# A decoder step on one core: the entry of layer 0 in one block, dilated attention by head pairs

## The chip, the core and the metric

The kernel runs on one core of one Trainium2 chip. The metric is device time in microseconds (us), as a median over runs. The core has a TensorE (PE) for matrix products, VectorE (DVE), ScalarE (ACT), GpSimd (POOL) and SyncE (SP), each with an instruction row of its own that runs in order; 16 DMA engines move data between DRAM and SBUF (128 partitions). TensorE writes its products into PSUM.

## The reference

One inference step of a two-layer decoder, for a prompt of 1024 tokens and a sample group of 8 sequences of 4 tokens, which share all weights (D_MODEL 1024, float32). Every sub-layer has a root-mean-square norm ahead and is added to its input.

```python
h = rmsnorm(x, norm_mix[layer])
# layer 0, ab_mix
a_lin, a_gate, q, k, v = split_cols(h @ w_in, AB_SPLITS)
a_out, conv_st = conv_module(a_lin * jax.nn.sigmoid(a_gate), conv_hist, ...)
q = rmsnorm(q.reshape(shp), qn)
k = rmsnorm(k.reshape(shp), kn)
for g, (window, dil) in enumerate(zip(WINDOWS, DILATIONS)):   # 128, 512, 2048 by 1, 4, 16
    s = jnp.einsum('nrbqhd,nrbkhd->nrbhqk', qb, kb).astype(F32) * HEAD_DIM ** -0.5 + bias
    s = jnp.where(mask[:, None], s, -jnp.inf)
    o = jnp.einsum('nrbhqk,nrbkhd->nrbqhd', jnp.exp(s - lse[..., None]), vb.astype(F32))
merged = jnp.concatenate([a_out, b_out...], axis=-1)   # @ w_out
```

The three groups of dilated attention have 4 heads of 64 each, blocks of 128 queries against their own and the previous block of keys, and are merged by the softmax of their log-sums. Outputs include the new window caches: for each of the 8 sequences and each group, the old cached keys and values shifted by the 4 new ones (up to 2 MB each in the third group). Layer 1 has gated linear attention beside an indexer-sparse attention with 8 heads: scores over all keys, of which the 256 best of an index stay. For the sample its past keys and values come in pages of 128 tokens. Each layer ends in a SwiGLU feed-forward net.

## The kernel before, in words

The residual stream lies transposed in SBUF: `S.xT`, eight channel tiles k of 128 by T = 1056 tokens, in the first eight rows of `home`. Large products run as three passes over high and low parts of both operands (`Parts`, `passes`), in three pieces of 352 columns (`multiply_pairs`, L364); every weight comes as a raw slice of 512 KB, whose high part ScalarE makes (L336) and whose low part VectorE or GpSimd (L340), with two slots j. The semaphore `W.free[j]` says that slot j of PSUM may be written, `W.product[j]` that its product is done. Small products are plain float32, which count as two TensorE instructions each in the trace; a transpose counts as one.

The program is a chain of blocks. In a block each engine has a hand-written program and they meet in semaphores; between blocks there is a barrier. The order of each row is the order of the code, and DMAs are issued in it from SP's or ScalarE's row.

The entry of layer 0 is four blocks. `load_inputs` (L168) loads the input rows (`xrow`, nine tiles) and 15 small gains on SP, turns x by channel tiles once all rows are in (L205), and copies to `xT` (L217). `bias_lines` (L543) forms relative-position bias lines by a product with one-hot rows (L573, L576), keeps them (L583, L585), stores them, and issues their spread to 128 rows each in DRAM, from which Toeplitz tables are read later. `rms_norm` (L235) squares on ScalarE (L262), sums over channels with a matrix of ones (L284), takes logarithm and exponential (L267, L269), multiplies on VectorE (L307), and splits h in high (L272) and low part, the low parts by turns on VectorE (L301) and GpSimd (L294). The ring between them holds two channel tiles. `glu_products` (L599) turns conv taps and history (L623, L628), then runs four pairs of products; ScalarE takes the sigmoid of slot 0 (L637), VectorE multiplies (L651 to L656).

`qkv_products` (L675) makes q and k of 12 head pairs, one per period, copied by ScalarE (L736), with weights loaded on SP (L328) and the convolution on VectorE (L765 to L772); then the values. `dilated_prompt` (L998) goes over 24 blocks (group g, query block b), 13 of which have one key tile and 11 two. Per block TensorE does scores (L1043), transposes of the probabilities (L1056) and value products (L1066), VectorE the bias (L1083), the row maximum (L1088) and the copy out (L1074), ScalarE the exponentials (L1101) and the copy of the turned probabilities (L1120). ScalarE also issues one cache copy per block (L1113), and SP stores each block's partial rows (L1030), of which four lie in a ring. `dsa_sample` (L2634) has two halves of four sequences each: 16 groups of pages are turned and scored (L2770, L2779), and at a half's end come the new keys and the biases:

```python
                if q % N_PAGES == N_PAGES - 1:
                    ...
                    new_keys_and_bias(q // N_PAGES)      # L2786 to L2793
            turn_probs(0)                                # L2799, L2800
            weigh_values(0)                              # L2810, L2814
            turn_probs(1)
            weigh_values(1)
            turn_out(0)                                  # L2819
```

VectorE takes each half's maximum (L2707), copies turned probabilities (L2711) and adds up heads (`own_heads`, L2721). SP loads pages into the slots that the value products have freed (L2475).

## Time and profile before

| | us |
|---|---|
| three runs | 3776.13, 3785.69, 3785.43 (median 3785.43) |
| the profiled execution: its own time, its span | 3779.81, 3778.0 |
| PE busy (share of the span) | 3154.7 (84%) |
| PE weight loads | 2899.2 (77%) |
| DVE | 1734.0 (46%) |
| ACT | 905.8 (24%) |
| POOL | 128.2 (3%) |

The program has 47856 instructions and moves 257.11 MB. A timeline row gives start, duration, engine, line of the kernel, operation, output<-input and count, and in brackets the engine's idle time before it and what ended that. SPq and ACTq rows are DMA issues. A window row gives each engine's busy time in a stretch and the granted clock of TensorE, where 1.00 is 2.4 GHz and 0.50 is 1.2 GHz. A row of waits gives total us, times and the longest.

### The profile page before, as it was taken

To read this page: it belongs to the slowest core of one execution; us is meant where nothing else is said; L and a number is where in the kernel's file an instruction comes from. 1 tells how busy PE (TensorE), PEld (TensorE's weight loads), DVE (VectorE), ACT (ScalarE), POOL (GpSimd) and SP (SyncE) were. 2 spreads that over 40 slices of the span, in tenths; PEclk is the share of its full clock that TensorE was granted. 3 is DMA by queue.
4 is the path that set the end of the run, shared out by engine and by line. 5 is a ranking of instruction groups with operands and counts; after the bars stand their busy time and mean duration, and the time that the engine had idled before them with its cause. 6 is when DMAs were issued, how large, how long until landed. Compare 5 with 4: busy or idle time off the path is not lost. (4 is left out here: it accounts for less than half of the span.)

```text
span 3778.0 us, 47856 instructions
## 1 busy us (share of the span) xinstructions
PE 3154.7 (84%) x19536; PEld 2899.2 (77%) x19552; DVE 1734.0 (46%) x2434; ACT 905.8 (24%) x1380; POOL 128.2 (3%) x53
## 2 busy tenths in 40 slices
PE   4689778325999999999689844569987999999999
PEld 2689756224999999999479834445664999999998
DVE  1269623453433232333499869373323333232333
ACT  1225324201321111113211141234521322111110
POOL 0112100000000000000012100000000000000000
PEclk7899976655999999999799955679987999999999
DMA  5111137373111111112111000114074111111111
GB/s 180 39 39 39 45 106 247 122 205 96 50 45 50 45 44 45 45 42 82 28 47 48 17 7 13 34 39 131 1 215 151 45 45 45 45 44 45 45 44 69
DMA packets 304496, 257.11 MB, mean 68 GB/s; under 512 B 31313, under 2 KB 279218, under 8 KB 303322
## 3 DMA queue, kind: packets, MB, share of 16 engines
q1 hardware_dynamic: 298079, 223.42, 20.0%
q10 hardware_dynamic: 6300, 32.12, 2.6%
q8 instruction: 75, 1.23, 0.1%
q14 instruction: 42, 0.34, 0.0%
HBM read 226.72 MB, written 62.64 MB: 77 GB/s over the span
## 5 line engine op out<-in xcount | busy, mean ns | idle before, releaser
L364 PE MATMUL ps<-h_given,w_parts_given 128*128 128x352 f32 x6048 | 979.8, 323 | 0.0
L364 PEld LDWEIGHTS ps<-h_given,w_parts_given 128*128 128x128 f32 x6048 | 979.0, 188 | 0.0
L364 PE MATMUL ps<-hidden_ffn,w_parts_given 128*128 128x352 f32 x4176 | 684.2, 326 | 21.2 <-DVE w_parts_given L340 21.2
L364 PEld LDWEIGHTS ps<-hidden_ffn,w_parts_given 128*128 128x128 f32 x4176 | 682.3, 190 | 22.1 <-issue 22.1
L340 DVE TENSOR_TENSOR w_parts_given<-w_given,w_parts_given 128x1024 fp32r<-128x1024 f32 (+2 forms) x154 | 181.9, 1181 | 626.2 <-ACT w_parts_given L336 626.2
L336 ACT ACTIVATE w_parts_given<-w_given 128x1024 fp32r<-128x1024 f32 (+2 forms) x154 | 158.0, 1026 | 914.5 <-PE ps L364 870.8
L1543 DVE TENSOR_TENSOR home<-home,ps 128x1056 f32<-128x1056 f32 (+1 forms) x64 | 80.3, 1254 | 430.4 <-PE ps L364 406.9
L364 PE MATMUL ps<-h_given,w_parts_cd 128*128 128x352 f32 x1152 | 188.4, 325 | 9.7 <-POOL w_parts_cd L340 9.7
L364 PEld LDWEIGHTS ps<-h_given,w_parts_cd 128*128 128x128 f32 x1152 | 188.1, 190 | 9.8 <-issue 9.8
L1998 DVE MATCH_REPLACE8 work<-best,work 128x1024 f32<-128x1024 f32 (+2 forms) x192 | 165.4, 864 | 0.0
L1991 DVE MAX8 best<-work 128x8 f32<-128x1024 f32 (+2 forms) x192 | 154.8, 865 | 0.0
L770 DVE SCALAR_TENSOR_TENSOR yT<-uT,taps,yT 128x1024 f32<-128x1024 f32 x120 | 152.9, 1274 | 0.0
L452 PE MATMUL ps<-h,w_parts_qk 128*128 128x352 f32 x720 | 121.8, 329 | 0.0
L452 PEld LDWEIGHTS ps<-h,w_parts_qk 128*128 128x128 f32 x720 | 116.8, 188 | 4.8 <-issue 4.8
L1502 ACT ACTIVATE hidden_ffn<-home 128x1056 f32 (+1 forms) x44 | 47.8, 1087 | 228.2 <-DVE home L1556 228.2
L792 PE MATMUL ps<-w_parts_qk,h 128*128 128x256 f32 (+1 forms) x648 | 84.2, 295 | 19.0 <-issue 13.8
L792 PEld LDWEIGHTS ps<-w_parts_qk,h 128*128 128x128 f32 (+1 forms) x648 | 82.6, 193 | 21.2 <-issue 14.3
L364 PE MATMUL ps<-h,w_parts_glu 128*128 128x352 f32 x576 | 95.3, 328 | 0.0
L364 PEld LDWEIGHTS ps<-h,w_parts_glu 128*128 128x128 f32 x576 | 95.1, 192 | 0.0
L792 PE MATMUL ps<-w_parts_dv,h_given 128*128 128x256 f32 (+1 forms) x432 | 55.0, 292 | 38.7 <-DVE w_parts_dv L340 35.1
L2540 PEld LDWEIGHTS ps<-diag_dsa,sc_dsa 128*128 128x128 f32 x576 | 70.2, 191 | 21.8 <-issue 20.2
L2540 PE MATMUL ps<-diag_dsa,sc_dsa 128*128 128x128 f32 x576 | 85.3, 289 | 0.2 <-DVE diag_dsa L2596 0.2
(413 smaller groups left out, 3574.8 us busy)
## 6 DMA issues: line engine op xcount, KB each, us to landing
kv_early<-in_cache_dsa_kv SPq DMA_DIRECT2D x92, 256.0 KB, 3.1
w_given<-in_w_ffn_gate SPq DMA_DIRECT2D x44, 512.0 KB, 3.8
w_given<-in_w_ffn_up SPq DMA_DIRECT2D x44, 512.0 KB, 3.8
w_given<-in_w_ffn_down SPq DMA_DIRECT2D x32, 448.0 KB, 3.7
w_cd<-in_w_in_cd SPq DMA_DIRECT2D x20, 512.0 KB, 4.0
w_qk<-in_w_in_ab SPq DMA_DIRECT2D x18, 512.0 KB, 3.8
kv_late<-in_cache_dsa_kv SPq DMA_DIRECT2D x36, 256.0 KB, 3.1
x_spill<-home SPq DMA_DIRECT2D x2, 4224.0 KB, 16.4
```

Of the source, the lines that this page charges most:

```text
L336: act.activation(self.parts.hi[:, 0:kt, j, :], self.raw[:, 0:kt, j, :], ACT.Copy).then_inc(self.hi_made[j], 1)
L340: eng.tensor_tensor(self.parts.lo[:, 0:kt, j, :], self.raw[:, 0:kt, j, :], self.parts.hi[:, 0:kt, j, :], ALU.subtract).then_inc(self.lo_ma ...
L364: last = pe.matmul(S.ps[:, j * 1536 + at:j * 1536 + at + size], w[:, k, j, :], x[:, k, t:t + size], start=k == 0 and n == 0, stop=k == kt ...
L452: last = pe.matmul(S.ps[:, j * 1536 + at:j * 1536 + at + size], w[:, k, j, :], x[:, k, t:t + size], start=k == 0 and p == 0, stop=k == KD ...
L770: dve.scalar_tensor_tensor(yT[:, c, 0:SEQ], uT[:, c, t:t + SEQ], taps[:, c, t:t + 1], yT[:, c, 0:SEQ], ALU.mult, ALU.add).then_inc(conv_st ...
L792: last = pe.matmul(vps[0:m, n % 2, 0:GW], tokens(g, b, x[:, k, :]), w[:, k].rearrange("p j c -> p (j c)"), start=k == 0 and i == 0, stop=k ...
L1502: act.activation(hidden.hi[:, bass.ds(i, 1), :].rearrange("p a t -> p (a t)"), whole, ACT.Copy).then_inc(hi_made, 1)
L1543: dve.tensor_tensor(x, x, slot(S, j), ALU.add).then_inc(W.free[j], 1)
L1991: dve.max(self.best[0:self.rows[j], j, :], line).then_inc(step, 1)
L1998: dve.match_replace(line, self.best[0:self.rows[j], j, :], line, TAKEN).then_inc(step, 1)
L2540: last = pe.matmul(t_ps[:, g % 2, i * P:(i + 1) * P], sc[:, u % 3, b, kt * P:(kt + 1) * P], diag[:, u % 2, b, :], start=True, stop=True)
```

## The change

- **Entry.** The four blocks become one, `entry`. Rows of x are turned, copied, squared and summed by token tiles t, each with a semaphore of its own for its load. Bias-line products come next, then the norm, all of it on VectorE, then the gated products; the first pair follows the low parts k by k. Conv history and taps are turned behind each pair. ScalarE issues the loads of the bias table, the gain of this norm, the one-hot lines and the history at its start, and 13 loads of the other gains behind the high parts, ahead of the first `W.free[0]`. The gated products are unrolled loops. SP stores and spreads the lines between weight loads.
- **q/k products.** ScalarE issues two cache copies per head pair (`copy_cache`), and waits for them at the block's end.
- **Dilated attention.** The unit of turning, copying and weighing is half a block (two heads): turning is a product with the identity, the ring of turned probabilities has four halves instead of two wholes, the value products stand one unit behind, and the cache copies are gone.
- **Sample's sparse attention.** The second half's new keys and biases stand behind the first half's value products; its maximum stands behind `own_heads(0)`.

```diff
...
+def entry(nc, S, W, rows, uT, taps, vS, yT):
...
+            sp.dma_start(S.dsa_line, line_d).then_inc(lines_out, 16)
+            load_weight_pairs(sp, W, KD, CC, w_cols(w, CONV_CH), w_cols(w, 0), there=1)
...
+            def transpose(t):
+                n = N[t]
+                pe.wait_ge(x_in[t], 16)
+                if t >= 2:
+                    pe.wait_ge(evacuated, t - 1)
+                for k in range(KD):
+                    last = pe.transpose(x_ps[:, t % 2, k, 0:n], rows[0:n, t, k * P:(k + 1) * P], S.ident[0:n, 0:n])
+                last.then_inc(transposed, 1)
+            def sum_squares(t):
+                n = N[t]
+                pe.wait_ge(squared, t + 1)
+                for k in range(KD):
+                    last = pe.matmul(sum_ps[:, t * P:t * P + n], S.ones[:, :], sq[:, t % 2, k, 0:n], start=k == 0, stop=k == KD - 1)
+                last.then_inc(summed, 1)
+            pe.wait_ge(ident_in, 16)
+            pe.wait_ge(ones_made, 1)
+            for t in range(QT + 1):
+                transpose(t)
+                if t:
+                    sum_squares(t - 1)
+            sum_squares(QT)
...
+            last.then_inc(lines_product, 1)
+            pe.wait_ge(lines_kept, 2)
+            pe.wait_ge(mean_ready, 1)
+            pe.wait_ge(hist_in, 48)
...
+                multiply_pairs(pe, S, W, KD, 1, S.h, c, made=made_in_order(lo_made, 0) if c == 0 else None)
+                if c:
+                    pe.wait_ge(placed, c)
...
+                act.wait_ge(evacuated, t + 1)
+                if t >= 2:
+                    act.wait_ge(summed, t - 1)
+                act.activation(sq[:, t % 2, :, 0:n], S.xT[:, :, t * P:t * P + n], ACT.Square).then_inc(squared, 1)
...
+                act.activation(S.h.hi[:, k, :], normed[:, k % 2, :], ACT.Copy).then_inc(hi_made, 1)
+            act.dma_start(S.head_ones[:, :], S.c["head_ones"]).then_inc(gains_in, 16)
+            act.dma_start(S.g_mix[:, 1, :], S.d["norm_mix"][1].rearrange("(k p) -> p k", p=P)).then_inc(gains_in, 16)
+            for layer in range(2):
+                act.dma_start(S.g_ffn[:, layer, :], S.d["norm_ffn"][layer].rearrange("(k p) -> p k", p=P)).then_inc(gains_in, 16)
+            for i, name in enumerate(("qn_ab", "kn_ab", "qn_cd", "kn_cd")):
+                for half in range(2):
+                    act.dma_start(S.g_qk[half * DH:(half + 1) * DH, i:i + 1], S.d[name].rearrange("a d -> d a")).then_inc(gains_in, 16)
+            act.dma_start(S.g_gla[:, :], S.d["gla_norm"].rearrange("a v -> v a")).then_inc(gains_in, 16)
+            act.sem_inc(W.free[0], 1)
+            for i in range(CC):
+                if i + 1 < CC:
+                    W.high(act, 0, i + 2, KD)
...
+            dve.wait_ge(rstd_ready, 1)
+            for k in range(KD):
+                if k >= 2:
+                    dve.wait_ge(lo_made, k - 1)
+                dve.scalar_tensor_tensor(normed[:, k % 2, :], S.xT[:, k, :], S.g_mix[:, 0, k:k + 1], rstd, ALU.mult, ALU.mult).then_inc(normalised, 1)
+                if k:
+                    low_part(k - 1)
+            low_part(KD - 1)
+            dve.sem_inc(W.free[1], 1)
...
+def copy_cache(act, S, g, n, out):
+    name, cache = ("win128_s", "win512_s", "win2048_s")[g], S.d[("cache_win128", "cache_win512", "cache_win2048")[g]][0]
+    old = cache.shape[1]
+    keep = min(WINDOWS[g], old + L_NEW) - L_NEW
+    act.dma_start(S.o[name][0, n, 0:keep].rearrange("t a h d -> t (a h d)"),
+                  cache[n, old - keep:old].rearrange("t a h d -> t (a h d)")).then_inc(out, 16)
...
+                for g, n in (divmod(2 * u, N_SEQ), divmod(2 * u + 1, N_SEQ)):
+                    copy_cache(act, S, g, n, cache_out)
...
-        pT = sb("pT", [P, 2, HPG, 256])
+        pT = sb("pT", [P, 4, 2, 256])
...
+            def turn_probs(u):
+                i, f = divmod(u, 2)
+                kts = 2 if has_previous(*blocks[i]) else 1
+                pe.wait_ge(exps, u + 1)
+                if u >= 2:
+                    pe.wait_ge(kept, u - 1)
+                for b in range(2):
+                    for kt in range(kts):
+                        last = pe.matmul(t_ps[:, f, b, kt * P:(kt + 1) * P], sc[:, i % 3, place(2 * f + b), kt * P:(kt + 1) * P], S.ident[:, :],
+                                         start=True, stop=True)
+                last.then_inc(turned, 1)
+            def weigh_values(u):
+                i, f = divmod(u, 2)
+                g, b = blocks[i]
+                kts = 2 if has_previous(g, b) else 1
+                pe.wait_ge(kept, u + 1)
+                if i >= 2 and f == 0:
+                    pe.wait_ge(sums_copied, i - 1)
+                for h in (2 * f, 2 * f + 1):
+                    for kt in range(kts):
+                        v = vS[:, g, b - (kts - 1) + kt, h * DH:(h + 1) * DH]
+                        last = pe.matmul(o_ps[:, i % 2, h * DH:(h + 1) * DH], pT[:, u % 4, h % 2, kt * P:(kt + 1) * P], v,
+                                         start=kt == 0, stop=kt == kts - 1)
+                if f:
+                    last.then_inc(summed, 1)
             scores(0)
             scores(1)
-            for i, (g, b) in enumerate(blocks):
-                pe.wait_ge(exps, i + 1)
-                if i:
-                    pe.wait_ge(kept, i)
-                kts = 2 if has_previous(g, b) else 1
-                for h in range(HPG):
-                    for kt in range(kts):
-                        last = pe.transpose(t_ps[:, h, kt * P:(kt + 1) * P], sc[:, i % 3, place(h), kt * P:(kt + 1) * P], S.ident[:, :])
-                last.then_inc(turned, 1)
-                if i + 2 < len(blocks):
-                    scores(i + 2)
-                pe.wait_ge(kept, i + 1)
-                if i >= 2:
-                    pe.wait_ge(sums_copied, i - 1)
-                for h in range(HPG):
-                    for kt in range(kts):
-                        v = vS[:, g, b - (kts - 1) + kt, h * DH:(h + 1) * DH]
-                        last = pe.matmul(o_ps[:, i % 2, h * DH:(h + 1) * DH], pT[:, i % 2, h, kt * P:(kt + 1) * P], v,
-                                         start=kt == 0, stop=kt == kts - 1)
-                last.then_inc(summed, 1)
+            for u in range(2 * len(blocks)):
+                turn_probs(u)
+                if u % 2 and u // 2 + 2 < len(blocks):
+                    scores(u // 2 + 2)
+                if u:
+                    weigh_values(u - 1)
+            weigh_values(2 * len(blocks) - 1)
...
+            def exponentials(u):
+                i, f = divmod(u, 2)
+                kts = 2 if has_previous(*blocks[i]) else 1
+                if f == 0:
+                    act.wait_ge(row_in, i + 1)
+                for h in (2 * f, 2 * f + 1):
                     last = act.activation(sc[:, i % 3, place(h), 0:kts * P], sc[:, i % 3, place(h), 0:kts * P], ACT.Exp,
                                           bias=row[:, i % 4, h, AT_M:AT_M + 1], accum_out=row[:, i % 4, h, AT_L:AT_L + 1])
-                    if h == HPG - 1:
-                        last.then_inc(exps, 1)
+                last.then_inc(exps, 1)
...
+            def keep_probs(u):
+                i, f = divmod(u, 2)
+                kts = 2 if has_previous(*blocks[i]) else 1
+                act.wait_ge(turned, u + 1)
+                if u >= 4:
+                    act.wait_ge(summed, i - 1)
+                act.activation(pT[:, u % 4, :, 0:kts * P], t_ps[:, f, :, 0:kts * P], ACT.Copy).then_inc(kept, 1)
...
-                name, cache = ("win128_s", "win512_s", "win2048_s")[g], S.d[("cache_win128", "cache_win512", "cache_win2048")[g]][0]
-                old = cache.shape[1]
-                keep = min(WINDOWS[g], old + L_NEW) - L_NEW
-                act.dma_start(S.o[name][0, b, 0:keep].rearrange("t a h d -> t (a h d)"),
-                              cache[b, old - keep:old].rearrange("t a h d -> t (a h d)")).then_inc(cache_out, 16)
...
+            exponentials(1)
+            for u in range(2 * len(blocks)):
+                i, f = divmod(u, 2)
+                if u + 2 < 2 * len(blocks):
+                    exponentials(u + 2)
+                keep_probs(u)
...
-            maximum(1)
             dve.wait_ge(consts, 48)
             keep_probs(0)
+            own_heads(0)
+            maximum(1)
...
-                if q % N_PAGES == N_PAGES - 1:
-                    if q < N_PAGES:
-                        pe.wait_ge(tables_made, 1)
-                        pe.wait_ge(consts, 48)
-                        pe.wait_ge(hot_in, 32)
-                    new_keys_and_bias(q // N_PAGES)
+                if q == N_PAGES - 1:
+                    pe.wait_ge(tables_made, 1)
+                    pe.wait_ge(consts, 48)
+                    pe.wait_ge(hot_in, 32)
+                    new_keys_and_bias(0)
             turn_probs(0)
             weigh_values(0)
+            new_keys_and_bias(1)
...
```

TensorE's row at the entry, before (transposes of x, bias lines, sums over squares, history and taps, first gated pair):

```order
L205 MATMUL ps<-ident,xrow 128x128 x8
L205 MATMUL ps<-ident,xrow 128x32
...
L573 MATMUL ps<-hot,tab 4x383 x2
L573 MATMUL ps<-hot,tab 4x255
L576 MATMUL ps<-hot_dsa,tab 8x512 x2
L576 MATMUL ps<-hot_dsa,tab 8x127
...
L284 MATMUL ps<-vS,ones 128x352 x24
...
L623 MATMUL ps<-ident,home 128x31 x4
L628 MATMUL ps<-ident,home 128x120 x8
...
L364 MATMUL ps<-h,w_parts_glu 128x352 x144
```

And now:

```order
L495 MATMUL ps<-ident,x_rows 128x128 x16
L502 MATMUL ps<-vS,ones 128x128 x8
L495 MATMUL ps<-ident,x_rows 128x128 x8
L502 MATMUL ps<-vS,ones 128x128 x8
...
L517 MATMUL ps<-yT,tab 4x383 x2
L517 MATMUL ps<-yT,tab 4x255
L519 MATMUL ps<-yT,tab 8x512 x2
L519 MATMUL ps<-yT,tab 8x127
...
L234 MATMUL ps<-h,w_parts_glu 128x352 x144
...
L529 MATMUL ps<-ident,home 128x120 x2
L530 MATMUL ps<-ident,home 128x31
```

Sums stand between the transposes of x, and the history behind the pair.

ScalarE's row at the entry, before (squares, first weights' high parts, logarithm and exponential, high parts of h):

```order
L262 ACTIVATE vS<-home 128x1056 x8
L336 ACTIVATE w_parts_glu<-w_glu 128x8x128 x2
L267 ACT_TABLE_LOAD
L267 ACTIVATE vS<-ps,eps 128x1056
L269 ACT_TABLE_LOAD
L269 ACTIVATE vS<-vS 128x1056
L272 ACTIVATE h<-vS 128x1056 x8
...
L336 ACTIVATE w_parts_glu<-w_glu 128x8x128
```

And now:

```order
L547 ACTIVATE vS<-home 128x1024 x8
...
L206 ACTIVATE w_parts_glu<-w_glu 128x8x128 x2
...
L552 ACTIVATE vS<-ps,eps 128x1056
...
L554 ACTIVATE vS<-vS 128x1056
L557 ACTIVATE h<-vS 128x1056 x8
L559 DMA head_ones<-const_head_ones 128x128
L560 DMA g_mix<-in_norm_mix 128x8x1
L562 DMA g_ffn<-in_norm_ffn 128x8x1 x2
L565 DMA g_qk<-in_qn_ab 64x1 x2
...
L566 DMA g_gla<-in_gla_norm 128x1
L206 ACTIVATE w_parts_glu<-w_glu 128x8x128
```

The gain loads, on SP's row before, stand between the high parts of h and the next weights.

TensorE at the start of the dilated attention, before (scores, turning, values by block):

```order
L1043 MATMUL ps<-home 128x128 x4
L1043 MATMUL ps<-home 128x256 x4
L1056 MATMUL ps<-ident,sc 128x128 x4
L1043 MATMUL ps<-home 128x256 x4
L1066 MATMUL ps<-vS,pT 128x64 x4
L1056 MATMUL ps<-ident,sc 128x128 x8
```

And now, by pair of heads:

```order
L1010 MATMUL ps<-home 128x128 x4
L1010 MATMUL ps<-home 128x256 x4
L1022 MATMUL ps<-ident,sc 128x128 x4
L1010 MATMUL ps<-home 128x256 x4
L1036 MATMUL ps<-vS,pT 128x64 x2
L1022 MATMUL ps<-ident,sc 128x128 x4
L1036 MATMUL ps<-vS,pT 128x64 x2
L1022 MATMUL ps<-ident,sc 128x128 x4
L1010 MATMUL ps<-home 128x256 x4
L1036 MATMUL ps<-vS,pT 128x64 x4
```

Between a turn and its values there now stands the next turn.

TensorE at the end of the sample's sparse attention, before (last scores, new keys and biases, turning, values):

```order
L2779 MATMUL ps<-kT,qb_dsa 32x128 x32
L2786 MATMUL ps<-home,qb_dsa 32x32 x16
L2788 MATMUL ps<-dsa_other,ident 128x32
L2792 MATMUL ps<-hot_s,tabr_dsa 128x512 x4
L2793 MATMUL ps<-work_s,dsa_rows 128x512
...
L2799 MATMUL ps<-ident,work 128x128 x8
...
L2810 MATMUL ps<-kv_early,pT_s 32x512 x4
L2810 MATMUL ps<-kv_late,pT_s 32x512 x12
L2810 MATMUL ps<-kv_early,pT_s 32x512 x16
L2814 MATMUL ps<-dv_new,pT_s 32x512 x4
L2799 MATMUL ps<-ident,work 128x128 x8
```

And now:

```order
L2759 MATMUL ps<-kT,qb_dsa 32x128 x32
L2779 MATMUL ps<-ident,work 128x128 x8
...
L2790 MATMUL ps<-kv_early,pT_s 32x512 x4
L2790 MATMUL ps<-kv_late,pT_s 32x512 x12
L2790 MATMUL ps<-kv_early,pT_s 32x512 x16
L2794 MATMUL ps<-dv_new,pT_s 32x512 x4
L2766 MATMUL ps<-home,qb_dsa 32x32 x16
L2768 MATMUL ps<-dsa_other,ident 128x32
L2772 MATMUL ps<-hot_s,tabr_dsa 128x512 x4
...
L2773 MATMUL ps<-new_taken,dsa_rows 128x32
L2779 MATMUL ps<-ident,work 128x128 x8
```

The rows of new keys and biases moved from ahead of the first turn to behind the first values.

## Rows read from the trace of the kernel before

**Rows 1.** Timeline of the entry: start us, us, engine, operation, count, idle before.
```profile
47.65 1.34 DVE L583 COPY line<-ps 4x383 f32<-4x383 f32 x3 [11.43 <-PE ps L576]
...
90.89 2.55 DVE L307 SCALAR_TENSOR_TENSOR vS<-home,g_mix,vS 128x1056 f32<-128x1056 f32 x2 [40.64 <-ACT vS L269]
...
127.39 95.32 PE L364 MATMUL ps<-h,w_parts_glu 128*128 128x352 f32 x576
...
141.22 1.28 ACT L336 ACT_TABLE_LOAD   x1 [28.82 <-PE ps L364]
...
222.75 0.19 DVE L651 TENSOR_TENSOR uT<-ps,home 128x32 f32<-128x32 f32 x1 [19.64 <-PE ps L364]
```

**Rows 2.** Dilated attention: timeline; window with clock, DMA share; waits; issues and landing.
```profile
528.34 2.95 SPq L1024 DMA_DIRECT2D toep<-ab_copies  x6
...
567.49 1.14 PE L1043 MATMUL ps<-home 64*128 64x256 f32 x8
...
576.96 1.04 PE L1056 MATMUL ps<-ident,sc 128*128 128x128 f32 x8
...
580.06 2.00 PE L1066 MATMUL ps<-vS,pT 128*128 128x64 f32 x16
...
680.67 0.50 PEld L1350 LDWEIGHTS ps<-yT,ones 128*128 128x128 f32 x2 [7.52 <-issue]
...
610.00:636.00 26.00, 26.00 (x129) 22.27 (x127) 10.09 (x15) 12.41 (x46) 0.00 (x0) 0.50 0.92 309
...
DVE part_row L1088 <- DMA part_rows<-part_row: 18.9, 3, 12.1
...
L1113 ACTq DMA_DIRECT2D out_win_s<-in_cache_win x24: 517/517/641, 536.0 to 665.8; - x24
...
DMA to landing us min/median/max: 2.8/5.6/14.2
...
DMA to landing us min/median/max: 1.5/3.5/18.4
```

**Rows 3.** Timeline, end of the sample's sparse attention, and SyncE's page loads.
```profile
2825.39 0.49 PE L2786 MATMUL ps<-home,qb_dsa 128*32 128x32 f32 x32
...
2841.77 1.97 PE L2799 MATMUL ps<-ident,work 128*128 128x128 f32 x8
...
2845.52 1.94 PE L2810 MATMUL ps<-kv_early,pT_s 128*32 128x512 f32 x8 [1.57 <-DVE pT_s L2712]
...
2879.06 1.93 PE L2814 MATMUL ps<-dv_new,pT_s 32*32 32x512 f32 x8
...
2830.68 2.57 SPq L2475 DMA_DIRECT2D kv_early<-in_cache_dsa_kv  x3
...
2848.24 1.45 SPq L2475 DMA_DIRECT2D kv_early<-in_cache_dsa_kv  x2
```

**Rows 4.** DMA issues (KB each, median us to landing), and timeline of SyncE's queue.
```profile
xrow<-in_x_prompt SPq DMA_DIRECT2D x8, 512.0 KB, 7.3
...
12.49 4.26 SPq L185 DMA_DIRECT2D g_ffn<-in_norm_ffn  x2
...
16.80 1.23 SPq L188 DMA_DIRECT2D g_qk<-in_qn_ab  x2
```

**Rows 5.** Timeline of TensorE in the prompt's sparse attention.
```profile
2564.08 2.05 PE L2540 MATMUL ps<-diag_dsa,sc_dsa 128*128 128x128 f32 x16 [0.18 <-DVE diag_dsa L2596]
```

**Rows 6.** Windows: stretch, busy us PE PEld DVE ACT POOL, clock, DMA, GB/s.
```profile
16.00:36.00 20.00, 13.29 (x72) 10.80 (x72) 9.68 (x9) 0.00 (x0) 0.00 (x0) 1.00 0.08 1
...
40.00:48.00 8.00, 7.40 (x12) 1.40 (x12) 0.35 (x1) 0.00 (x0) 0.00 (x0) 0.50 0.00 0
```

**Rows 7.** Timeline of the q/k products: ScalarE's copies and a weight load.
```profile
272.32 1.05 ACT L736 ACTIVATE home<-ps 128x1056 f32<-128x1056 f32 x1 [5.58 <-PE ps L452]
...
277.90 0.37 SPq L328 DMA_DIRECT2D w_qk<-in_w_in_ab  x1
...
285.66 1.05 ACT L736 ACTIVATE home<-ps 128x1056 f32<-128x1056 f32 x1 [5.58 <-PE ps L452]
```

In the second group the first row on landing is that of the cache copies, the second that of the stores of partial rows.

333 lines of the change are left out of this document (115 added, 218 removed).

## The prediction

> **What bounds the kernel now.** The busy shares in the table above say TensorE, 84% busy, but a share is an average over stages, so I read the places that the diff touches: the timeline of the entry (before 223 us), of the dilated attention and of the end of the sparse attention for the sample, then the DMA issues, windows over the entry, and the q/k products. All times are of the profiled execution, whose own time is 3779.81 over a span of 3778.0; the median of the three runs is 3785.43, 0.15% above it. With their spread (3776 to 3786) that makes about 0.3% the least change that a measurement of this kernel can tell from none.
>
> In the entry TensorE waits for a chain of blocks: the first gated product starts at 127.39 and ends at 141.2, and from there the products run on until 222.75 [rows 1]. What moves their start moves the rest one for one. In the dilated attention TensorE is busy all through 610 to 636 at a granted clock of 0.50, with DMA at 0.92, and VectorE waits 12.1 us once for a store of partial rows [rows 2]. In the sample's sparse attention the last value pages are asked for one by one as slots come free [rows 3].
>
> **Entry.** Four blocks become one, and transposes, squares and sums go by token tiles of 128 instead of by channel tiles. I rebuild the chain. The first row tile is in at about 5: a tile is 512 KB, and eight issued together had a median of 7.3 us to landing [rows 4], the first well under that. Before, TensorE waited for all nine. A tile then costs 8 transposes and 8 float32 sums. Eight transposes took 1.04 [rows 2]; a float32 product counts as two instructions, and 16 of 128 columns took 2.05 in another place [rows 5]. That is 3.1 per tile, 25 for eight, and about 4 for the first tile's copy and square and the short tile, which nothing hides: the sums end at 34. This needs the upper clock level (2.4 GHz). It stood at 1.00 over 16 to 36 with transposes alone [rows 6]; at 0.50 the tiles would cost 6 each, 20 us more in all.
>
> The Trainium skill (TensorE: Matmul & The Clock Gate, Part 4: PE-mode transpose) says the full clock level doesn't engage for transpose mode. By it the sum would be 20 us longer here. The window with transposes alone at 1.00 [rows 6] differs, and the measurement decides.
>
> The bias-line products, 12 instructions, took 7.40 at 0.50 [rows 6], so about 4 at full clock; I take 5, to 39. VectorE copies them, 1.34 for the three narrow ones [rows 1] and as much for the wide one: to 42. The logarithm and the exponential on ScalarE run beside this and end no later. The norm is now on VectorE alone: two multiplies take 2.55 [rows 1], and a subtraction has the same size, so 1.27 each. The eighth multiply is the 14th instruction of its row: 42 + 14 x 1.27 = 60. TensorE could follow the low parts from 44.5 on, were it not for a new gate. ScalarE frees slot 0 only behind the eighth high part, for which it waits until that multiply, and behind the issues of 13 gain loads. Two loads of 1024 single words took 4.26 to issue, two half columns 1.23 [rows 4], so 3 x 2.1 + 8 x 0.62 + 1.0 = 12.3 us, to 72. Nothing hides them: TensorE waits there, with VectorE done at 62.
>
> The first product then takes 13.8 as before, since TensorE comes to it from rest in both kernels: to 86, where it was 141.2, so 55 earlier. The history transposes, formerly ahead of the products, stand behind each pair, 4 x 0.9 of the gain back. Net **-52**. Bounds: -68 if the gate doesn't bind (the product follows the low parts and ends at 69), -58 if ScalarE's issues cost half, -32 if the tiles run at 0.50.
>
> The spill of x, the copies of the lines to DRAM (12 lines by 128 rows, 6.8 MB) and their issues stand on SP's queue around weight loads that are needed a pair of products later; I cost them at nothing. If a weight load came late behind them, it would be a few us.
>
> **q/k products.** The 24 cache copies move here from the attention, two per product, on ScalarE's queue. ScalarE idles 5.58 us of each 13.34 us period [rows 7], so 2 x 0.52 of issue (0.517 is each copy's [rows 2]) is free. Bandwidth is the question. The 2 MB copies of the third group fall in the last four products: 4.2 MB per 13.34 us is 315 GB/s, against 309 at a DMA share of 0.92 over 610 to 636 [rows 2]; so the DMA engines are about full there. A weight load issued at 277.90 is needed two products on, some 21 us later [rows 7]: hidden unless both copies stay ahead of it. Cost 0 to 30; I take **+1**, near the lower end, because the attention's own small stores landed in 3.5 at the median beside the same copies [rows 2].
>
> The Trainium skill (DMA: Bandwidth & Descriptors, Queues, rings and completion order) says each engine switches between its queues only where a packet ends. The slowest store of partial rows beside the copies, 18.4 us [rows 2], agrees. By the page a load of many small packets moves one packet for one of the copy's, which is the slower rival below.
>
> **Dilated attention.** The unit of work is now a pair of heads, and the value products trail by one pair, so a PSUM copy no longer stands between a turn and its product. The 140 transposes become full float32 products, twice the instructions. At full clock, for a block with two key tiles: turning 16 instructions, 2.05 where 8 took 1.04 before; scores 1.14; values 2.00 [rows 2, 5]: 5.2 us. One with one key tile: 1.0 + 0.7 + 1.0 and some 0.4 of wait on VectorE and ScalarE, 3.1. With 11 and 13 of them 57 + 40 = 97. Ahead of it come 2.95 for the issue of six tables from 528.34 on [rows 2], about 3 for their landing, and a bias, a maximum and first exponentials of about 1 each: 8.6 by estimate, and 3 for a cold start; behind it 5 for the last store. 528 + 114 = 642, where the next stage began at 680.7 [rows 2]: **-38**. Of that 18.9 us are the three waits for stores of partial rows [rows 2], which go with the copies; the rest is overlap. Bounds: -45 if the blocks overlap perfectly, +35 if TensorE stays at 0.50: 11 x 9.6 + 13 x 5.2 + 14 = 187. I take full clock, since the same mix of products in the prompt's sparse attention ran at 16 in 2.05 us [rows 5].
>
> The Trainium skill speaks against this change. The page TensorE: Matmul & The Clock Gate, Terms, gives transpose mode as four times as fast as a float32 product. By it the turns would cost 4.2 per large block and this stage would gain nothing. The rows have 1.04 for 8 transposes against 2.05 for 16 instructions, twice [rows 2, 5].
>
> **Sparse attention of the sample.** The new keys and the biases of the second half (2825.39 to 2841.77, 16.4 us [rows 3]) move behind the first half's value products, and its maximum too. The turn and the copy between took 3.75, so the values start at 2829, not 2845.5. SP's loads stop with the row that ends at 2833.25 and go on at 2848.24 [rows 3]: the last pages come up to 15.0 us sooner. TensorE's own chain is longer: 72 value instructions, 8 in 1.94 from rest [rows 3], half of that once the clock is up, 9 in all, to 2838; biases to 2854.4; maximum and exponentials 2.7 (two passes over 1056 columns of about 1.3 each), turn and copy 3.75, to 2861; then eight less than 72 at full clock, 8, to 2869. Before, the last eight began at 2879.06 [rows 3]: 2868.5 is **-11**. Bounds: -15 (the pages' gain) and -6 (the clock low in the last part).
>
> **Sum:** -52 + 1 - 38 - 11 = -100, 3779.8 - 100 = 3680.
>
> **Rivals.** *Half clock in the attention* (8%). A mix of row-paired scores and 64-column value products may not lift it. For it: 0.50 through 610 to 636 with TensorE full [rows 2]. Against: the prompt's sparse attention, with the same kinds of product at full speed [rows 5]. The stage takes 187, not 114: 3680 + 73 = 3753.
>
> *The entry gives less* (13%). Half clock over the tile loop, +20: 3700. For: every turn and sum waits a little for VectorE or ScalarE. Against: 1.00 over 16 to 36 with waits of that kind in it, 13.29 busy of 20 [rows 6].
>
> *The cache copies stall the weights* (11%). Two 2 MB copies in a period leave under 1 us for a load. Copies took up to 14.2 us to land [rows 2], more than a period. If four loads each come 10 us late, that is 20 to 40 with what the slack takes: 3710.
>
> *Turning costs four times a transpose* (4%). The turning product has 128 columns and a new stationary each time, so its weight load may not be hidden in this order. Each large block pays 2.1 more, each small one 1.05, 37 in all: 3717.
>
> *The other side: slower than before* (2%). One mechanism: in the last q/k products each small packet of a weight load waits for one large packet of a copy. A store with 8 small packets per engine took up to 18.4 us to land [rows 2], 2.3 each; a load has 64 per engine, so 147 us, some 125 past its slack. One such load gives 3805. It decides from about 110 us of waiting on; the copies have so few packets per engine for 2 MB that their queue should run dry first.
>
> *The gate doesn't bind* (2%), 3664. *The change doesn't do what it says* (2%): attention and value pages gain nothing, 3729.
>
> **How the numbers follow.** The forecast case has 58%: 3680, its own range 3662 to 3700. With the cases at 3664, 3700, 3710 and 3717 it makes 88%; of these the edges lose a few, and the 80% range is 3655 to 3722. Faster by over 0.3% (under 3774) 0.97; within 0.3% 0.01; slower 0.02.
>
> **What would show it.** First gated product at 72, behind ScalarE's gain loads, its end at 86; clock 1.0 over 5 to 35. A period of 13.3 in the q/k products and no waits on weight loads. Attention 114 long at a clock of 0.9 or more, no wait on a store of partial rows. Last value products of the sample 11 earlier against the stage's start. It is wrong if the clock stays at 0.50 in either of the first places, if the first product starts before 60, or if the period of the q/k products grows past 14.

## The result, and the profile after

The changed kernel took 3676.68 us (median of four, 3672.13 to 3683.80) where the kernel before took 3784.14; the ratio is 0.9718 (95% interval 0.9702 to 0.9734), 2.8% faster. The forecast was 3680, range 3655 to 3722. Ratios compare runs in the fast state; one execution of the run with products by whole blocks took 8860.04 us and is left out of its ratio. The profiled execution took 3673.23 over a span of 3671.4, 106.6 less than before's span.

The page after, its first lines (busy us, share of the span, instructions):

```profile
span 3671.4 us, 48370 instructions
PE 3136.7 (85%) x19788; PEld 2899.6 (79%) x19788; DVE 1733.5 (47%) x2444; ACT 899.3 (24%) x1400; POOL 116.8 (3%) x49
```

TensorE's busy time fell by only 18 us (3154.7 to 3136.7); the rest of the 106.6 us is waiting that went. Where it was won is read off by the start of the same work in both traces:

| place | before | after | earlier by | forecast for the step |
|---|---|---|---|---|
| last gated product kept | 222.75 [rows 1] | 164.06 | 58.7 | 52 |
| dilated attention, first scores | 528.40 | 469.12 | 59.3 | -1, for a step of 0.6 |
| next stage, first sums | 680.70 | 582.60 | 98.1 | 38, for a step of 38.8 |
| end of the span | 3778.0 | 3671.4 | 106.6 | 11, for a step of 8.5 |

The entry after, from the timeline (columns as in [rows 1]):

```profile
5.09 1.94 PE L495 MATMUL ps<-ident,x_rows 128*128 128x128 f32 x8 [5.09 <-DMA x_rows<-in_x_prompt]
...
9.66 3.62 PE L502 MATMUL ps<-vS,ones 128*128 128x128 f32 x16
...
27.70 1.96 PE L502 MATMUL ps<-vS,ones 128*128 128x128 f32 x16
...
33.96 1.88 PE L517 MATMUL ps<-yT,tab 33*4 33x383 f32 x6
...
40.48 2.53 DVE L602 SCALAR_TENSOR_TENSOR vS<-home,g_mix,vS 128x1056 f32<-128x1056 f32 x2
...
58.18 0.36 ACTq L559 DMA_DIRECT2D head_ones<-const_head_ones  x1
...
59.06 1.23 ACTq L562 DMA_DIRECT2D g_ffn<-in_norm_ffn  x2
...
65.55 0.60 ACTq L566 DMA_DIRECT2D g_gla<-in_gla_norm  x1
66.29 26.10 PE L234 MATMUL ps<-h,w_parts_glu 128*128 128x352 f32 x144 [28.51 <-ACTq L567]
...
80.83 1.06 ACT L206 ACTIVATE w_parts_glu<-w_glu 128x1024 fp32r<-128x1024 f32 x1 [21.57 <-PE ps L234]
...
164.06 0.19 DVE L613 TENSOR_TENSOR uT<-ps,home 128x32 f32<-128x32 f32 x1 [19.73 <-PE ps L234]
```

The first tile was in at 5.09 and the bias-line products began at 34, as in the forecast's chain; the sums of a tile cost 3.62 at first and 1.96 later. Behind the bias lines TensorE stood 28.51 us, and what ended that is ScalarE's queue at L567, the release of slot 0 behind the gain loads. The windows show its clock (columns as in [rows 6]):

```profile
0.00:20.00 20.00, 14.04 (x91) 13.68 (x92) 5.26 (x8) 5.52 (x5) 0.41 (x5) 1.00 0.92 273
20.00:40.00 20.00, 17.78 (x139) 14.62 (x138) 7.41 (x10) 11.34 (x11) 4.65 (x2) 0.95 0.61 231
40.00:66.00 26.00, 0.00 (x0) 0.00 (x0) 20.34 (x18) 8.66 (x8) 0.00 (x0) 0.50 0.30 68
```

The 1.00 of the first row isn't to be trusted. In the kernel before, the same column shows 1.00 from 0 to 16, where TensorE has done nothing yet, and its transposes there tell another clock. Timeline of TensorE, kernel before:

```profile
16.28 4.35 PE L205 MATMUL ps<-ident,xrow 128*128 128x128 f32 x18 [16.28 <-DMA xrow<-in_x_sample]
...
31.04 2.46 PE L205 MATMUL ps<-ident,xrow 128*128 128x128 f32 x18 [0.16 <-DVE home L217]
```

The same 18 transposes took 4.35 us at first and 2.46 us later, so the first ran at the lower level. In the changed kernel the lower level held up to the third tile at 13.07: eight transposes took 1.94 and 1.97 (1.04 later), 16 sums 3.62 (1.96 later).

In the q/k products the period stayed 13.34 us as in [rows 7], with the copies issued beside them. Timeline of ScalarE, then the landing times of the weights from the tile's view; the slowest took 13.1 us (4.9 before), within the slack of some 21:

```profile
321.70 1.05 ACT L700 ACTIVATE home<-ps 128x1056 f32<-128x1056 f32 x1 [5.58 <-PE ps L322]
...
335.04 1.05 ACT L700 ACTIVATE home<-ps 128x1056 f32<-128x1056 f32 x1 [5.58 <-PE ps L322]
```

```profile
DMA to landing us min/median/max: 3.7/4.0/13.1
```

The dilated attention after, windows, where before had 0.50 with a DMA share of 0.92 [rows 2]:

```profile
490.00:510.00 20.00, 20.00 (x168) 18.02 (x168) 11.83 (x14) 12.49 (x41) 0.00 (x0) 1.00 0.08 29
...
550.00:570.00 20.00, 20.00 (x155) 18.19 (x155) 10.32 (x18) 12.93 (x59) 0.00 (x0) 1.00 0.10 35
```

And its TensorE rows, with the loads and last products of the sample's attention, from the timeline:

```profile
469.12 2.93 PE L1010 MATMUL ps<-home 64*128 64x128 f32 x16 [8.70 <-PEq L949]
...
500.10 1.11 PE L1022 MATMUL ps<-ident,sc 128*128 128x128 f32 x8
501.13 1.13 PE L1010 MATMUL ps<-home 64*128 64x256 f32 x8
502.20 1.10 PE L1036 MATMUL ps<-vS,pT 128*128 128x64 f32 x8
...
582.60 9.03 PE L1330 MATMUL ps<-yT,ones 128*128 128x352 f32 x24 [2.72 <-PEq L968]
...
2720.35 20.56 SPq L2455 DMA_DIRECT2D kv_early<-in_cache_dsa_kv  x19
...
2754.92 8.38 SPq L2455 DMA_DIRECT2D kv_early<-in_cache_dsa_kv  x8
...
2763.51 5.22 PE L2790 MATMUL ps<-kv_early,pT_s 128*32 128x512 f32 x24 [1.50 <-DVE pT_s L2692]
```

SP no longer stands, as it did between 2833.25 and 2848.24 [rows 3]: its last row of loads ends at 2763.3, ahead of the second half's values at 2763.51, and no value product waits for a page. Before, TensorE waited for pages four times in the second half's values (2863.46 to 2877.20), 10.9 us in all.

### The profile page after: what moved, and what is told of

It reads as the page before. It is cut to its first block and busy times, and to the rows that moved or that the text cites. A ratio compares the mean times of both kernels' runs of the same rounds, so it can differ in the third digit from the quotient of the medians.

```text
span 3671.4 us, 48370 instructions
## 1 busy us (share of the span) xinstructions
PE 3136.7 (85%) x19788; PEld 2899.6 (79%) x19788; DVE 1733.5 (47%) x2444; ACT 899.3 (24%) x1400; POOL 116.8 (3%) x49
## 5 line engine op out<-in xcount | busy, mean ns | idle before, releaser
L234 PE MATMUL ps<-hidden_ffn,w_parts_given 128*128 128x352 f32 x4176 | 683.6, 326 | 24.3 <-DVE w_parts_given L210 24.3
L759 PEld LDWEIGHTS ps<-w_parts_dv,h_given 128*128 128x128 f32 (+1 forms) x432 | 54.1, 191 | 39.7 <-issue 39.5
```

Of the source, the lines that this page charges most:

```text
L234: last = pe.matmul(S.ps[:, j * 1536 + at:j * 1536 + at + size], w[:, k, j, :], x[:, k, t:t + size], start=k == 0 and n == 0, stop=k == kt ...
L759: last = pe.matmul(vps[0:m, n % 2, 0:GW], tokens(g, b, x[:, k, :]), w[:, k].rearrange("p j c -> p (j c)"), start=k == 0 and i == 0, stop=k ...
```

## The experiments

All were timed beside the kernel before; "ratio" is to it, and a hundredth of a per cent is 0.38 us. The length of the dilated attention is from its first scores to the next stage's first sums, in the profiled execution. Two executions of unchanged code can differ: with the same entry, the last gated product is kept at 164.06 in the changed kernel and at 160.58 in the run with the copies back in the attention, whose tile loop is at full speed from 9.4 us on. Line numbers of an experiment are its own.

**The gate in the entry.**

```diff
         def _(act):
+            act.sem_inc(W.free[0], 1)
             act.dma_start(S.tab[0:BUCKETS, :], ...
...
-            act.sem_inc(W.free[0], 1)
             for i in range(CC):
```

> The changed kernel, with the first release of slot 0 moved from behind the gain loads to the head of ScalarE's row; the loads stay where they are. In the changed kernel's trace the first gated product starts at 66.3, behind ScalarE's row of gain loads, while the first low part is there at 44.2 and the last at 60.5. Theory (the gate binds): the product starts at about 44 and follows the low parts, slot 0 is done at 62 and slot 1 at about 74, where it was 92.1; the whole is 18 us faster than the changed kernel, some 3659 against 3677. Rival (another limit stands right behind: VectorE's release of slot 1 at 60.5 and a TensorE clock that falls while it waits for each low part): the pair ends at 80 or later, the gain is 12 or less. Rival 2: the gate is not what TensorE waits for: no change.

Ratio 0.9668 (0.9652 to 0.9684), 3657.61 us: 19 us below the changed kernel. Timeline of TensorE, and a window (columns as in [rows 6]):

```profile
44.22 4.70 PE L234 MATMUL ps<-h,w_parts_glu 128*128 128x352 f32 x18 [6.54 <-DVE h L581]
...
59.26 14.83 PE L234 MATMUL ps<-h,w_parts_glu 128*128 128x352 f32 x90 [0.81 <-DVE h L581]
73.93 0.37 PE L529 MATMUL ps<-ident,home 120*128 120x120 f32 x2
```

```profile
40.00:62.00 22.00, 14.27 (x71) 12.85 (x72) 20.23 (x18) 8.67 (x8) 0.00 (x0) 0.83 0.34 80
```

TensorE follows VectorE's low parts, waiting up to 0.8 us for each, and the pair ends at 73.9, where the changed kernel had 92.4. The theory holds; what limits TensorE behind the gate is VectorE, from 44 to 59.

**Where the gains are loaded.**

```diff
             sp.dma_start(rows[0:TS, QT, :], S.d["x_sample"].rearrange("n l d -> (n l) d")).then_inc(x_in[QT], 16)
+            sp.dma_start(S.head_ones[:, :], S.c["head_ones"]).then_inc(gains_in, 16)
+            sp.dma_start(S.g_mix[:, 1, :], S.d["norm_mix"][1].rearrange("(k p) -> p k", p=P)).then_inc(gains_in, 16)
...
-            act.dma_start(S.head_ones[:, :], S.c["head_ones"]).then_inc(gains_in, 16)
-            act.dma_start(S.g_mix[:, 1, :], S.d["norm_mix"][1].rearrange("(k p) -> p k", p=P)).then_inc(gains_in, 16)
...
             act.sem_inc(W.free[0], 1)
```

> The changed kernel, with the 13 gain loads taken from ScalarE's row and put on SP's behind the eight large loads of x, where they stood before. In the kernel before two such loads of 1024 words took 4.26 and 5.99 us to issue there, on ScalarE's row in the changed kernel 1.23 for two. Theory (the issue is short in itself, and was long since the queue was full of large loads): the two-load rows of gains take 4 us again on SP. The gate then opens behind the last high part, at 59, the first product starts at 60 to 61, and the whole is 5 to 6 us faster than the changed kernel. Rival (the price belongs to the engine or the order): they take 1.2 on SP too. Rival 2: the first weights come late behind them, and the entry gains nothing.

Ratio 0.9701 (0.9684 to 0.9718), some 7 us below the changed kernel, with intervals that overlap. The trace is sharper: the first product starts at 58.50, the last is kept at 156.45, 7.6 earlier. SP's timeline:

```profile
7.31 15.49 SPq L467 DMA_DIRECT2D g_ffn<-in_norm_ffn  x2
22.84 1.23 SPq L470 DMA_DIRECT2D g_qk<-in_qn_ab  x2
```

The same two loads take 1.23 us on an idle queue (L562 after), 4.26 in [rows 4], and 15.49 here. In the changed kernel two weight loads in the same place behind x took 10.45, and 1.05 later. So the long rows belong to the place behind 4 MB of x and not to the loads, as the theory has it, though 15.49 is far over its 4. The loads of g_qk, whose size was right, took 1.2 to 1.3 in all three. The forecast's 12.3 us for the gate, built on the row of 4.26, was really 8.0. What fills the queue, bytes or packets, no run separates: 24 cache copies with far more bytes took 0.61 each to issue (below).

**GpSimd's share of the norm**, on top of the early release and of transposes (below).

```diff
+            for k in range(1, KD, 2):
+                pool.wait_ge(hi_made, k + 1)
+                pool.tensor_tensor(S.h.lo[:, k, :], normed[:, k % 2, :], S.h.hi[:, k, :], ALU.subtract).then_inc(lo_made_odd, 1)
```

> The changed kernel with the early release of slot 0, transposes in the dilated attention, and the odd low parts of the norm back on GpSimd. With the release alone the first product followed low parts that VectorE finished every 2.52 us, from 44.2 to 60.5. Theory (VectorE's row sets that pace): two multiplies and one subtraction per two channel tiles make 3.9 in place of 5.0 us, the last low part comes 3 to 4 us sooner, and the whole is 3642 to 3643. Rival (GpSimd's subtraction, 2.3 us per weight slice where VectorE takes 1.2, and its share of the SBUF port set the pace): no gain, or up to 3 us slower.

Ratio 0.9649 (0.9633 to 0.9665), 5 us slower than without it (0.9635, below), with intervals that overlap. In the traces the first pair ends at 78.62, and at 74.26 without it, 4.4 later. The rival holds. The timeline:

```profile
44.16 2.44 POOL L489 TENSOR_TENSOR h<-vS,h 128x1056 fp32r<-128x1056 f32 x1 [8.26 <-ACT h L565]
44.17 4.76 DVE L611 SCALAR_TENSOR_TENSOR vS<-home,g_mix,vS 128x1056 f32<-128x1056 f32 x2
...
47.74 2.32 ACT L565 ACTIVATE h<-vS 128x1056 fp32r<-128x1056 f32 x2 [3.66 <-DVE vS L611]
...
50.13 2.44 POOL L489 TENSOR_TENSOR h<-vS,h 128x1056 fp32r<-128x1056 f32 x1 [3.54 <-ACT h L565]
```

Two multiplies take 4.76 beside GpSimd's subtraction and 2.53 without it. ScalarE has the first of them only at 47.74, 3.6 us after its start and 1.1 after the subtraction's end. Two channel tiles take 5.97 us (44.16 to 50.13) where VectorE alone needs 5.04. The kernel before had this too, with 5.95 us for two tiles; putting the whole norm on one engine was a part of the change's gain, by estimate 8 x 0.47 = 3.7 us.

**Transposes in the dilated attention.**

```diff
-                        last = pe.matmul(t_ps[...], sc[:, i % 3, ...], S.ident[:, :], start=True, stop=True)
+                        last = pe.transpose(t_ps[...], sc[:, i % 3, ...], S.ident[:, :])
```

> The changed kernel, with the turning product of the dilated attention made a transpose again; the order by head pairs stays. Theory A (a transpose costs half of the float32 product, and the clock is set by TensorE being busy at all): 140 transposes of 0.13 us in place of 280 instructions of 0.13, the stage loses up to 18 of its 113.5 us. Theory B (transposes are what held the clock at 0.50 in the kernel before): the granted clock of the stage falls to 0.5 to 0.7, scores and values take twice as long, and the stage is 10 to 50 us longer than with the products. The Trainium skill (TensorE: Matmul & The Clock Gate, Part 4: PE-mode transpose) speaks for B.

Ratio 0.9684 (0.9668 to 0.9700), 10 us by the medians and 13 by the ratios faster than the changed kernel; the stage is 104.1 long (469.56 to 573.64), 9.4 shorter. The groups of the lines view, of this kernel, and then of the changed one:

```profile
L1022 PE MATMUL ps<-ident,sc 128*128 128x128 f32 x140 | 25.0, 288 | 6.8 <-ACT sc L1082 6.7
```

```profile
L1022 PE MATMUL ps<-ident,sc 128*128 128x128 f32 x280 | 43.1, 292 | 6.6 <-ACT sc L1083 6.6
```

One window of this kernel:

```profile
510.00:530.00 20.00, 18.87 (x126) 14.69 (x126) 9.87 (x14) 12.98 (x51) 0.00 (x0) 1.00 0.10 34
```

Half of the instructions, at the same mean, and the clock is 1.00 with transposes in the mix. Theory A's outcome holds for this order, theory B's does not. That transposes don't matter for the clock in any order is not shown by it, and the runs by whole blocks below show otherwise.

**The cache copies back in the attention.**

```diff
+                if f == 0:
+                    copy_cache(act, S, *blocks[i], cache_out)
```

> The changed kernel, with the 24 cache copies back in the dilated attention, one per block on ScalarE's row, and gone from the q/k products. Theory (18.9 us of the 38 were waits for stores of partial rows beside the copies): those waits come back, 15 to 20 us slower than the changed kernel, and the q/k products stay within 2. Rival (with faster blocks the same copies have less time to land, so the waits grow): 25 to 45 slower. Rival 2 (order by pairs alone brings the gain, the waits are covered): under 5.

Ratio 0.9796 (0.9779 to 0.9812), 28 to 30 us slower than the changed kernel; the stage is 147.0 long (467.32 to 614.34). Waits and two windows of the stage:

```profile
DVE part_row L1066 <- DMA part_rows<-part_row: 24.3, 2, 12.4
```

```profile
550.00:570.00 20.00, 12.64 (x96) 11.21 (x94) 4.62 (x8) 6.39 (x28) 0.00 (x0) 0.88 0.98 328
570.00:590.00 20.00, 15.53 (x77) 14.19 (x78) 6.84 (x12) 9.08 (x40) 0.00 (x0) 0.52 0.85 292
```

The outcome is the first rival's: with faster blocks the same copies have less time, DMA is at 0.98, the waits for stores grow from 18.9 to 24.3, and the clock is at 0.52 behind them.

**One thing at a time in the kernel before.** The first moves only the copies, the second only replaces transposes by products, the third does both; the order stays by whole blocks. The copies' edit, and the turning's:

```diff
+                for g, n in (divmod(2 * u, N_SEQ), divmod(2 * u + 1, N_SEQ)):
+                    copy_cache(act, S, g, n, cache_out)
...
-                        last = pe.transpose(t_ps[:, h, kt * P:(kt + 1) * P], sc[...], S.ident[:, :])
+                        last = pe.matmul(t_ps[:, h, kt * P:(kt + 1) * P], sc[...], S.ident[:, :], start=True, stop=True)
```

> The kernel before, with nothing but the 24 cache copies moved into the q/k products, two per head pair; the dilated attention keeps its order by whole blocks with transposes. Theory (waits for stores behind the copies, and the clock that falls with them, are most of the gain): 20 to 28 us faster than before; the copies cost the q/k products nothing. Rival (the order by pairs brings it): under 10 us.

> The kernel before, with the transposes of the dilated attention made float32 products with the identity; order by whole blocks and cache copies as before. Theory A (the clock falls by TensorE's waits, of which there is one per block behind a PSUM copy, and transposes don't matter for it): the clock stays near what it was (0.5 to 0.8), the turns cost 10 to 25 us more. Theory B (transposes don't count for the clock, as the Trainium skill has it in TensorE: Matmul & The Clock Gate, Part 4: PE-mode transpose): the clock rises to 0.9 and more and the stage is 5 to 20 us shorter.

> The kernel before, with the cache copies moved into the q/k products and the transposes of the dilated attention made products; the order by whole blocks stays. With the runs so far it separates order and clock: with transposes and moved copies this stage took 130.4 us at clocks of 0.5 to 0.83, in the changed kernel 113.5. Theory (the products lift the clock to 1.00, which pays back their own cost, and the waits behind the PSUM copy remain): 120 to 128 us, 24 to 32 below the kernel before. Rival (with a cost of 140 more instructions and the same waits nothing is won): 130 us or more.

Ratios 0.9941 (0.9924 to 0.9957), 0.9990 (0.9979 to 1.0001) and 0.9920 (0.9904 to 0.9937). Windows of the three in this order, all of the same stretch, the first run's last stretch too; behind the second run's window stand its waits for stores:

```profile
570.00:590.00 20.00, 16.93 (x109) 14.34 (x106) 8.93 (x12) 10.07 (x35) 0.00 (x0) 0.83 0.06 21
...
636.00:660.00 24.00, 19.72 (x94) 17.01 (x92) 8.07 (x14) 9.12 (x37) 0.00 (x0) 0.50 0.10 35
```

```profile
570.00:590.00 20.00, 18.40 (x140) 15.95 (x139) 9.17 (x12) 11.05 (x38) 0.00 (x0) 1.00 0.46 153
```

```profile
DVE part_row L1089 <- DMA part_rows<-part_row: 22.9, 4, 10.4
```

```profile
570.00:590.00 20.00, 18.39 (x140) 15.93 (x139) 9.16 (x12) 11.07 (x39) 0.00 (x0) 1.00 0.08 27
```

The lengths of the stage together:

| order, turning | copies beside | copies moved |
|---|---|---|
| blocks, transposes | 152.3 (before) | 130.4 |
| blocks, products | 151.2 | 125.1 |
| pairs, products | 147.0 | 113.5 (changed) |
| pairs, transposes | not run | 104.1 |

Copies moved alone: the theory's size holds, 22 us by the ratio and 21.9 in the stage, and no wait for a store is left. Its second half doesn't: the clock is 0.83, then 0.64 over 610 to 636 and 0.50 at the end, with DMA at 0.10. The 0.50 of before stood beside full DMA engines, but didn't come from them alone.

Products alone: neither theory holds whole. The clock is 1.00 from 550 to 636, with DMA up to 0.86, as theory B has it, but the stage is 1.1 shorter, not 5 to 20, since VectorE still waits 22.9 us for stores beside the copies.

Both: the theory holds, 125.1. With whole blocks, transposes leave the clock at 0.83 to 0.50 and products hold 1.00 (0.93 at the end), so the products win 5.3 us in spite of their number. By pairs, where the clock is 1.00 either way, transposes win 9.4. What in the order decides about the clock isn't shown. Where the copies stand beside, order and products together bring 5.3.

**The sample's sparse attention in the order of before.** The edit reverses the last two pieces of the diff.

> The changed kernel, with the sample's sparse attention in the order of before (both halves' new keys and biases ahead of the first turn, both maxima ahead of the first copies). Theory: 10 to 11 us slower than the changed kernel, as the shift between the two traces grows by 10.4 in this place. Rival (part of that shift is the clock's, from what stood ahead): 5 or less, or none.

Ratio 0.9738 (0.9722 to 0.9754), 8 us slower than the changed kernel by the ratios and 9 by the medians, with intervals that overlap. The trace is sharper. The scores ahead of the moved part start 2.9 us later here than in the changed kernel (2729.90 and 2727.01), the first turn of outputs 14.0 later (2787.99 and 2773.95), so the place is worth 11.1, and the theory holds. TensorE's timeline in the changed kernel, then in this one:

```profile
2727.01 2.03 PE L2759 MATMUL ps<-kT,qb_dsa 128*32 128x128 f32 x64
...
2773.95 0.33 PE L2799 MATMUL ps<-ident,out_rows 128*128 128x128 f32 x1
```

```profile
2729.90 2.03 PE L2759 MATMUL ps<-kT,qb_dsa 128*32 128x128 f32 x64
...
2787.99 0.47 PE L2799 MATMUL ps<-ident,out_rows 128*128 128x128 f32 x1
```

**All copies at once.**

```diff
-                for g, n in (divmod(2 * u, N_SEQ), divmod(2 * u + 1, N_SEQ)):
+                for g, n in [(g, n) for g in (2, 1, 0) for n in range(N_SEQ)] if u == 0 else ():
```

> The changed kernel, with all 24 cache copies issued one behind the other at the first q/k product, the largest first, instead of two per product. It puts the price on the rival that the copies stall the weights. Theory (ScalarE's row stands while its queue is full, as SP's did for 15.5 us behind 4 MB of x): 22 MB at about 150 GB/s each way hold ScalarE for some 100 us less what the queue takes; its copies out of PSUM then come late, and the whole is 60 to 120 us slower than the changed kernel. Rival (the queue takes all 24, weights and copies share the DMA engines by halves): weights land within their 21 us of slack, under 10 us slower.

Ratio 0.9872 (0.9855 to 0.9888), 58 us slower than the changed kernel. Timeline of ScalarE, and the weights' landing:

```profile
191.55 14.14 ACTq L634 DMA_DIRECT2D out_win_s<-in_cache_win  x22
...
275.89 1.06 ACT L206 ACTIVATE w_parts_qk<-w_qk 128x1024 fp32r<-128x1024 f32 x1 [51.88 <-DMA w_qk<-in_w_in_ab]
```

```profile
DMA to landing us min/median/max: 3.7/3.9/80.7
```

The size came out just under the theory's 60, and its mechanism was wrong: the queue took the 24 copies in 15.4 us (the row shows the last 22) and ScalarE went on, but one weight load, on SP's queue, took 80.7 us to land beside them. The copies themselves took at most 70.5, the last issued at 205.1, so the load, in at about 275.8, landed only when they were through. That is the prediction's rival of a load that moves at the copies' pace until their queue runs dry. It sets in between two copies per product (13.1 to landing) and 24 in a row. The Trainium skill (DMA: Bandwidth & Descriptors, Queues, rings and completion order) has each engine take turns between its queues packet by packet. The 80.7 is in keeping with that, but no run separates it from another way of sharing.

**The two improvements together:** the early release and transposes.

> The changed kernel with both the early release of slot 0 and transposes in the dilated attention. Theory (the two places are apart in time, so the gains add): 19 + 12 us, 3646 to 3649, 3.6% below the kernel before. Rival (the first stage's gain shifts the DMAs and clock of the second): 10 us less than that.

Ratio 0.9635 (0.9619 to 0.9651), 3645.72 us: 31 us below the changed kernel, about the sum of the two (19, and 10 to 13), so the theory holds. This beats both kernels.

## Why the prediction was right

The likeliest case came true, and the median lies 3.3 below the forecast. Step by step:

- **Entry:** 52 forecast, 58.7 measured. The gate's place and releaser were as told, and the chain to the norm was off by only 1.5 us (40.5 for 42). That is in part luck, since two errors of some 3 us each cancel. The forecast had full clock from the first tile on, as it read the 1.00 of [rows 6]; the changed kernel's first tiles ran at half, which costs about 3 by estimate from their rows. Later tiles took 2.67 each (16.16 to 18.83, L495), not 3.1. The term that was mis-sized is the issue of 13 gain loads: 12.3 forecast, 8.0 measured (58.2 to 66.2), since the row taken for the long ones, 4.26 for two, held a wait of the queue. TensorE started at 66.29, not 72, and slot 0 took 14.5 for 13.8. The history transposes between pairs cost 0.5 a pair, not 0.9. The bound of -58 "if ScalarE's issues cost half" is close to 58.7 by chance: the issues cost two thirds, and the rest came from the other terms.
- **q/k products:** 1 lost by the forecast, 0.6 gained in the table, period unchanged. The copies' own price is read between kernels that differ in them alone, from the last gated product kept to the attention's first scores. In the changed kernel that is 305.1 us with the copies and 306.7 without them (160.58 to 467.32), in the kernel before 306.5 with them (223.19 to 529.66) and 305.7 without. So the price lies within 2 us of nothing and not even its sign is shown; the forecast's 1 fits, and so would 0. The slowest weight landed in 13.1 of 21 us of slack.
- **Attention:** 38 forecast, 38.8 measured, full clock from 490 on, no wait for a store. The stage took 113.5 as forecast, with two errors of some 4 us that cancel: the blocks took 101.2 (478.68 to 579.87) for 97, the head and the tail 12.3 for 16.6. The gain's parts were not independent, as the forecast's "18.9 of waits, the rest overlap" has it. Moving the copies alone brings 21.9, pairs and products alone 5.3, both 38.8. What pairs and products save beside the copies is lost again to waits for stores (22.9 and 24.3 us in the two runs). And part of the rest is the clock, which the forecast gave no share: in whole blocks the products' full clock brings 5.3, and only the last 11.6 are the order. With transposes, once the copies are moved, the order by pairs brings 26.3 (130.4 to 104.1), the clock's rise to 1.00 included.
- **Turning:** the factor of two that the forecast took from the rows held (25.0 us for 140 instructions, 43.1 for 280). The forecast took the 140 extra instructions as a part of the change; against transposes in the same order they are 9.4 us of the stage.
- **Sample:** 11 forecast, 11.1 by the experiment. The chain held too: from the scores' end to the last eight value products it came to 43.1 by the forecast and to 44.0 in the trace (2728.96 to 2772.96). The table's 8.5 holds a drift in the stretch between, which has no edit: for the same instruction the changed kernel is 98.1 ahead at 582.60, about 94.5 from 895 to 1981, 92.4 at 2473, 96.6 at 2709, and 107.1 from 2821 on. The moved part lies between the last two. What causes the drift stays open.

The rivals: half clock in the attention didn't come (1.00 from 490 to 570). Half clock in the entry came for the first two tiles and a part of the third, and not beyond. The weights weren't stalled, and turning didn't cost four times a transpose.

## What to carry to other kernels

Take the price of a DMA issue from a row where its queue is empty, and look at what was issued ahead of it: the long issue rows here (4.26, 10.45, 15.49) all stood behind 4 MB of x. A release that stands behind unneeded issues on an in-order engine is a gate; put it where the resource is free, here worth 19 us. Move bulk copies out of a stage first, and only then judge its order: with the copies in place, pairs and products brought 5 us, without them 17. When a window shows the full clock in the first microseconds of a program, compare the durations of equal instructions before trusting it.

## What the runs showed that was not expected

- Products with the identity raised the clock from 0.83 and less to 1.00 in the order by whole blocks, and made the stage 9.4 us longer in the order by pairs. The Trainium skill (TensorE: Matmul & The Clock Gate, Part 4: PE-mode transpose) says that the full clock level doesn't engage for transpose mode, which doesn't count as busy in the same way. The first agrees. The 1.00 with transposes between products (510 to 530) does not, nor do the transposes alone of the kernel before, 18 of which took 2.46 us from 31.04 on.
- A GpSimd subtraction of 2.44 us beside VectorE's multiply kept the latter for 3.6 us where it takes 1.27 alone; it ended 1.1 us after the subtraction.
- Issuing 24 copies of up to 2 MB took ScalarE 15.4 us, 0.61 each, and one weight load beside them took 80.7 us to land.
- Moving bulk copies away took the waits for stores with it, but not the low clock of the stage beside them.
